# A transformer in one kernel: halves of a product placed by rule, rotary tables, a run of sums and the norms reordered

## The chip, the core and the metric

The kernel runs on one core of a Trainium2 chip. A core has TensorE (matmuls; PE in the rows, and PEld for its weight loads), VectorE (DVE), ScalarE (ACT), GpSimd (POOL) and SyncE (SP, which here only starts transfers); each works through its own queue of instructions in order and waits on semaphores. The metric is the device time of one execution in microseconds, the median of three runs.

## The reference

Two model blocks follow each other on 256 tokens of width 2048, all in fp32 from memory to memory; the output is the last layer norm's.

```python
def first_block(x, mem, ...):
    x = x + hybrid_mixer(x, ...)       # gated delta rule (8 heads) beside block attention (8 heads)
    x = x + cross_attention(x, mem, ...)
    x = x + conv_ffn(x, ...)           # (silu(conv(h @ w_gate) + b) * (h @ w_up)) @ w_down, d_ff 5632
    return rmsnorm(x, final_norm_g)

def second_block(x, positions, ...):
    cos, sin = _rope_tables(positions)
    for layer in range(2):
        if layer == 0:
            h = _mamba2_mixer(x, ...)  # in: 2048 -> 10304, 8 groups of a state-space model, out: 4096 -> 2048
        else:
            k_sh, v_sh = _shared_kv(x, kv_w, kv_b, cos, sin)
            h = _swa_mixer(x, k_sh, v_sh, cos, sin, ...)   # 32 heads of 64, window 128, rotary part of 16
        x = _layernorm(ALPHA * x + h, ln_g[layer], ln_b[layer])
    return x

def _rope_tables(positions):
    inv_freq = ROPE_THETA ** (-jnp.arange(0, ROT_DIM, 2, dtype=jnp.float32) / ROT_DIM)
    ang = positions.astype(jnp.float32)[..., None] * inv_freq
    return jnp.cos(ang), jnp.sin(ang)
```

## The kernel before

**Tiling.** Activations lie transposed in SBUF, as tiles of 128 features x 256 tokens (`XT[:, m, :]`). A weight matrix is read in chunks of 128 output features x 1024 rows, eight blocks k of 128 rows. SP loads a chunk into WR; ScalarE rounds it into WH (L1244); VectorE writes the rest, WR - WH, into WL (L1661). The moving operand is held the same way as XH and XL, or OH and OL. `half_of` then issues three matmuls for each block k, 128x128 weights against 128x256: L784 (XH, WH), L785 (XL, WH), L786 (XH, WL). There are 6144 such blocks, 18432 of the 20814 matmuls. The other matmuls are small steps between them: norms, transposes, attention, the state-space model's inner products.

**A split.** At the places in `OPENED`, 16 that are written out by hand, `in_two` issues the first matmul of a block as two with 128 columns (L760, L761). All 16 stand in some block of a stretch of products.

**The order.** `make_plan` writes one list of steps, and each engine issues its share of every step in that list's order. `product` appends the halves of a product, four blocks each, and after each calls `slot`, which takes a step from each small task that is due; `begin(task, names, gap, first)` enters such a task, with `gap` slots between its steps and `first` slots ahead. ScalarE's and VectorE's work on chunk i stands a fixed three chunks ahead of its use (AHEAD = 3).

**The program in order**, with the names of the products: gq, gk, gv, gz (delta rule), mq, mk, mv (attention), wo; xkv, xq, xo (cross attention); fg, fu, dn (feed-forward: 44 of fg and fu by turns, dn in four parts); a norm and dt; for each of eight groups g of the state-space layer sb, sc, x0 to x3, z0 to z3 and the steps "ssm" g (cb, x0, x1, ds, ..., y1, ns, nr); so, in four parts: 0 and 1 behind groups 2 and 4, 2 and 3 behind group 7; layer norm 0 with bkv (`three`); then 16 times wg and wq, one of each for a tile ti, beside the steps "swa" of tile ti - 1 (rope, lg, sm, sn, bk, pv); bo in two parts; layer norm 1 and the store.

**The steps that the change touches.** "rot" makes the rotary tables: seven steps on VectorE (L2238 to L2253 are five of their lines) and two Sin activations on ScalarE (L1562), begun ahead of so part 2; the tables lie in T2(0) and the scratch in T1(4) to T1(6) and T2(1). "mid" 1 sums the layer's input over its 16 tiles for the statistics: GpSimd copies (L2447) and adds (L2450), one in each slot from bkv 3 on, then "s". The rope of a product wq ti is four VectorE instructions (L2331) and two of GpSimd (L2637, L2640), and TensorE's attention of that tile (L1207, L1208) waits for them. "ln" is a layer norm: statistics ("stat"), TensorE's "sub", "rows" and "more", then "pair" 0 to 7, in which VectorE scales two tiles each (L2317). Some pairs get their mean subtracted ahead: in `centred` by VectorE (L2276, 128x512, for pairs 2, 8 and 14), by GpSimd for 10 and 12, and by TensorE for 4 and 6 (ln "sub"). In layer 0 ScalarE and GpSimd (L2630) also write XH and XL of the scaled tiles for the products bkv behind them.

## Time and profile before

| | |
|---|---|
| runs | 2455.44, 2456.77, 2457.15 us |
| median | 2456.77 us |
| the profiled execution | 2455.53 us, of which the span of the trace is 2453.5 us |
| busy | TensorE 98%, VectorE 72%, ScalarE 49%, GpSimd 21% |
| bytes moved | 418.29 MB, 170 GB/s |

Durations come from one profiled execution, which also marks when an instruction started and what the engine waited for. Matmuls are pipelined: the durations of TensorE's rows overlap, so what a matmul takes from the stream is the distance between two starts. The granted clock is the share of TensorE's full speed that the chip allowed.

### The profile page before, as it was taken

How to read it: one execution, taken by the hardware profiler on the slowest of the kernel's cores; microseconds unless marked ns; L12 is line 12 of the kernel's file. 1: busy time of each engine (PE TensorE's matmuls, PEld its weight loads, DVE VectorE, ACT ScalarE, POOL GpSimd, SP SyncE). 2: the span in 40 equal slices, each digit the busy share in tenths (PEclk: the TensorE clock that was granted, in tenths of full speed). 3: DMA queues.
4: the chain of work that ended last, by engine and by line, in shares of the span. 5: the costliest groups of instructions: out<-in, count | busy, mean ns of one | idle time of the engine just before them, and what ended most of it. 6: DMA issues, size and time to landing. Idle time of an engine off the chain costs nothing. (4 is left out here: it accounts for less than half of the span.)

```text
span 2453.5 us, 51551 instructions
## 1 busy us (share of the span) xinstructions
PE 2408.2 (98%) x20814; PEld 2367.7 (97%) x20814; DVE 1770.1 (72%) x2825; ACT 1211.1 (49%) x1918; POOL 505.7 (21%) x575
## 2 busy tenths in 40 slices
PE   7999999999999999999999999999999999999998
PEld 6999999999899999999999999999999999889998
DVE  6677646685666665655656888777887887888887
ACT  5433344554544444444444545544544554556554
POOL 1233310160200000000002312341221222521102
PEclk9999999999999999999999999999999999999999
DMA  6433335565555556556556645545554445444453
GB/s 216 157 126 123 123 125 178 186 205 168 163 189 192 197 177 209 195 179 211 191 179 190 195 161 170 172 165 171 171 178 158 163 151 183 151 154 157 157 166 117
DMA packets 124503, 418.29 MB, mean 170 GB/s; under 512 B 13796, under 2 KB 17644, under 8 KB 124012
## 3 DMA queue, kind: packets, MB, share of 16 engines
q1 hardware_dynamic: 124268, 415.00, 51.5%
q8 instruction: 167, 2.74, 0.5%
q14 instruction: 68, 0.56, 0.1%
HBM read 412.31 MB, written 3.68 MB: 170 GB/s over the span
## 5 line engine op out<-in xcount | busy, mean ns | idle before, releaser
L784 PE MATMUL b<-XH,WH 128*128 128x256 f32 x4213 | 1187.5, 282 | 21.9 <-DVE WL L1661 17.7
L785 PE MATMUL b<-XL,WH 128*128 128x256 f32 x4224 | 1173.9, 278 | 0.0
L786 PE MATMUL b<-XH,WL 128*128 128x256 f32 x4224 | 1173.3, 278 | 0.0
L1244 ACT ACTIVATE WH<-WR 128x1024 fp32r<-128x1024 f32 (+2 forms) x811 | 814.4, 1011 | 466.3 <-PE b L786 458.7
L1661 DVE TENSOR_TENSOR WL<-WR,WH 128x1024 fp32r<-128x1024 f32 (+2 forms) x811 | 993.3, 1235 | 14.5 <-ACT WH L1244 14.2
L784 PEld LDWEIGHTS b<-XH,WH 128*128 128x128 f32 x4213 | 793.4, 188 | 33.2 <-issue 17.0
L785 PEld LDWEIGHTS b<-XL,WH 128*128 128x128 f32 x4224 | 798.0, 189 | 0.6
L786 PEld LDWEIGHTS b<-XH,WL 128*128 128x128 f32 x4224 | 794.9, 188 | 0.0
L784 PE MATMUL b<-OH,WH 128*128 128x256 f32 x1675 | 468.4, 280 | 7.1 <-DVE WL L1661 5.7
L785 PE MATMUL b<-OL,WH 128*128 128x256 f32 x1680 | 466.5, 278 | 0.0
L786 PE MATMUL b<-OH,WL 128*128 128x256 f32 x1680 | 466.2, 278 | 0.0
L784 PEld LDWEIGHTS b<-OH,WH 128*128 128x128 f32 x1675 | 315.5, 188 | 10.6 <-issue 8.3
L785 PEld LDWEIGHTS b<-OL,WH 128*128 128x128 f32 x1680 | 316.0, 188 | 0.4
L786 PEld LDWEIGHTS b<-OH,WL 128*128 128x128 f32 x1680 | 315.8, 188 | 0.0
L1849 DVE TENSOR_TENSOR XT<-XT,b 128x256 f32<-128x256 f32 x192 | 80.5, 420 | 146.1 <-PE b L786 144.1
L1759 DVE SCALAR_TENSOR_TENSOR t1s<-cvs,par,t1s 128x256 f32<-128x256 f32 x304 | 153.0, 503 | 37.0 <-ACT t1s L1315 18.3
L1335 ACT ACTIVATE t1s<-t1s 128x256 f32<-128x256 f32 x156 | 64.8, 416 | 205.2 <-DVE t1s L1759 179.5
L2486 POOL TENSOR_TENSOR t2s<-t2s,RB 128x256 f32<-128x256 f32 x44 | 32.5, 739 | 559.9 <-DVE t2s L1787 559.9
L1807 DVE TENSOR_TENSOR cvs<-b,RB 128x256 f32<-128x256 f32 x116 | 48.7, 421 | 110.1 <-PE b L786 109.5
L2393 POOL TENSOR_TENSOR sms<-sms,con 128x2 f32<-128x2 f32 (+2 forms) x27 | 40.4, 1496 | 284.0 <-DVE sms L1980 98.0
L1787 DVE SCALAR_TENSOR_TENSOR t2s<-t1s 128x256 f32<-128x256 f32 x156 | 72.3, 464 | 8.3 <-ACT t1s L1335 8.3
L784 PE MATMUL b<-OX,WH 128*128 128x256 f32 x240 | 67.1, 279 | 0.0
(410 smaller groups left out, 2323.3 us busy)
## 6 DMA issues: line engine op xcount, KB each, us to landing
WR<-a_w_in SPq DMA_DIRECT2D x160, 512.0 KB, 3.7
WR<-w_in SPq DMA_DIRECT2D x112, 512.0 KB, 3.6
WR<-w_gate SPq DMA_DIRECT2D x88, 512.0 KB, 4.0
WR<-w_up SPq DMA_DIRECT2D x88, 512.0 KB, 4.1
WR<-a_w_out SPq DMA_DIRECT2D x64, 512.0 KB, 3.4
WR<-b_w_in SPq DMA_DIRECT2D x64, 512.0 KB, 3.7
WR<-w_down SPq DMA_DIRECT2D x64, 384.0 KB, 3.5
WR<-w_down SPq DMA_DIRECT2D x64, 320.0 KB, 2.9
```

What stands on the lines that cost most here:

```text
L784: mm(ps, WH[:, slot, at:at + P], xh, start=(k == 0), stop=False)
L785: mm(ps, WH[:, slot, at:at + P], xl, start=False, stop=False)
L786: m = mm(ps, WL[:, slot, at:at + P], xh, start=False, stop=(k == p["kt"] - 1))
L1244: act.activation(WH[:, s, 0:n], WR[:, r, 0:n], ACT.Copy).then_inc(*act_w.up(i))
L1335: act.activation(T1(2 + n % 2), T1(n % 2), ACT.Tanh, scale=0.5).then_inc(*act_cv.up("th", key))
L1661: dve.tensor_tensor(WL[:, s, 0:n], WR[:, r, 0:n], WH[:, s, 0:n].bitcast(F32), ALU.subtract).then_inc(*dve_w.up(i))
L1759: dve.scalar_tensor_tensor(y, b[:, j:j + S], pc(p["cw"], ci * K + j), y, ALU.mult, ALU.add).then_inc(*dve_cv.up("tap", key, j, also=("taps ...
L1787: dve.scalar_tensor_tensor(to, T1(2 + n % 2), 1.0, T1(n % 2), ALU.add, ALU.mult).then_inc(*dve_cv.up("end", key, also=("n", n)))
L1807: dve.tensor_tensor(cvs[:, p["c"] % 3, p["K"] - 1:p["K"] - 1 + S], ps, RB[:, :], ALU.mult).then_inc(*dve_ev.up(key))
L1849: dve.tensor_tensor(XT[:, m, :], XT[:, m, :], ps, ALU.add).then_inc(*dve_ev.up(key))
L2393: return pool.tensor_tensor(to[:, 0:n], columns[:, 0:n], cc("mhalf", 0, n), ALU.pow)
L2486: pool.tensor_tensor(gt[:, S:2 * S], gt[:, 0:S], RB[:, :], mult).then_inc(*pool_up.up(m))
```

## The change

**Splits.** `OPENED` goes. A new function `opened` reads the step list and puts one split into the second block of each stretch of product halves between small steps, if the stretch has at least 24 blocks, or at least 11 if the small step ahead of it is "ns", "sums" or a norm's. That gives 55 places, none of the old 16 among them.

**Rotary tables.** "rot" begins right behind norm 2, with a gap of 4, so its steps lie among the products fg and fu 0 to 3. The tables and the scratch move to parts of the constants that are no longer read (`turned`, "lev", "onehot"); so the waits at the first step are others.

**"mid" 1.** Gap 4 and first 24 in place of 1 and 1: a sum each product, from the loop of wg and wq on; "s" comes behind the last.

**Layer norms.** VectorE's `centred(8)` goes ahead, into "stat". GpSimd takes the root of the variance first and then its two sums, in layer 0 behind the XL parts of pairs 1 and 2. In layer 1 pair 14 gets its mean subtracted by TensorE, eight small matmuls (`ln`, "sub", 14), and `centred(14)` is gone there.

```diff
+        if layer:
+            self.step("ln", layer, "sub", 14)
...
-OPENED = {
-    (("gk", 0, 1), 4), (("gz", 1, 1), 12), (("gz", 2, 1), 12), (("gz", 3, 1), 12), (("xkv", 2), 8), (("fg", 0), 14),
-    (("fu", 0), 2), (("sc", 0), 8), (("x3", 0), 8), (("z1", 1), 4), (("z1", 4), 4), (("z1", 7), 4), (("so", 0, 14), 4),
-    (("so", 1, 14), 4), (("so", 2, 14), 4), (("bo", 0, 9), 4),
-}
...
+def opened(steps):
+
+    places, here, run, last = set(), None, 0, None
+    for step in [*steps, ("dt",)]:
+        if small(step):
+            sure = last is not None and (last[-1] in ("ns", "sums") or last[0] == "norm")
+            if here is not None and run >= (11 if sure else 24):
+                places.add(here)
+            here, run, last = None, 0, step
+        elif step[0] == "half":
+            key, k0, k1 = step[1], step[3], step[4]
+            if run == 0:
+                here = (key, k0 + 1)
+            run += k1 - k0
+    return places
...
     q.norm(2)
     q.late = False
+    q.begin(("rot",), ["a", "n0", "r0", "c0", "n1", "r1", "c1"], 4, 8)
...
-    q.begin(("rot",), ["a", "n0", "r0", "c0", "n1", "r1", "c1"])
...
-    q.begin(("mid", 1), [("x", m) for m in range(16)] + [None] * 12 + ["s"], 1, 1)
+    q.begin(("mid", 1), [("x", m) for m in range(16)] + [None] * 3 + ["s"], 4, 24)
...
-                if (key, k) in OPENED:
+                if (key, k) in plan.opened:
...
-            if m == 1:
-                w.wait_ge(*(pe_swa.of("lg", 15, 1) if layer else act_rot.of(1)))
+            if m == 1:
+                w.wait_ge(*(pe_swa.of("lg", 15, 1) if layer else pe_dt.of("t")))
...
                 centred(2)
+                centred(8)
...
-                    if 2 * j in (4, 6):
+                    if 2 * j in ((4, 6, 14) if layer else (4, 6)):
...
-                if j in (2, 5):
-                    centred(8 if j == 2 else 14)
+                if j == 5 and layer == 0:
+                    centred(14)
...
+                w.wait_ge(*dve_ln.of("ms", layer))
+                power(SM(21), SM(20)[:, 2:4], 2).then_inc(*pool_ln.up("r", layer))
                 w.wait_ge(*dve_ln.of("mu", layer))
-                for m in (10, 12):
...
+                if layer:
+                    centred(layer, 10)
+                    centred(layer, 12)
...
+                if j in (1, 2):
+                    centred(0, 8 + 2 * j)
```

In the order of the instructions, TensorE, behind the "nr" step of state-space group 4 (L747, in the changed kernel L778), where the stretch of 168 blocks begins; OH, OL are the moving operand's parts. Before:

```order
L786 MATMUL b<-OH,WL 128x256
L747 MATMUL b<-con,sms 128x128 x2
L784 MATMUL b<-OH,WH 128x256
L785 MATMUL b<-OL,WH 128x256
L786 MATMUL b<-OH,WL 128x256
L784 MATMUL b<-OH,WH 128x256
L785 MATMUL b<-OL,WH 128x256
L786 MATMUL b<-OH,WL 128x256
```

Now (L815 to L817 are L784 to L786, L791 and L792 are L760 and L761):

```order
L817 MATMUL b<-OH,WL 128x256
L778 MATMUL b<-con,sms 128x128 x2
L815 MATMUL b<-OH,WH 128x256
L816 MATMUL b<-OL,WH 128x256
L817 MATMUL b<-OH,WL 128x256
L791 MATMUL b<-OH,WH 128x128
L792 MATMUL b<-OH,WH 128x128
L816 MATMUL b<-OL,WH 128x256
L817 MATMUL b<-OH,WL 128x256
L815 MATMUL b<-OH,WH 128x256
```

The second block has its first matmul in two halves; the first block is as it was.

VectorE, in so part 2 behind the two t2s<-b,sms of group 7. Before:

```order
L2167 TENSOR_TENSOR t2s<-b,sms 128x512
L2238 SCALAR_TENSOR_TENSOR t1s<-t1s 128x256
L2240 SCALAR_TENSOR_TENSOR t1s<-t1s 128x256
L2242 SCALAR_TENSOR_TENSOR t1s<-t1s 128x256
L1849 TENSOR_TENSOR XT<-XT,b 128x256
L2249 TENSOR_SCALAR t1s<-t1s 128x256
L2251 TENSOR_TENSOR t1s<-t1s 128x256
L2249 TENSOR_SCALAR t1s<-t1s 128x256
L2251 TENSOR_TENSOR t1s<-t1s 128x256
L2253 TENSOR_SCALAR t1s<-t1s 128x256
L1661 TENSOR_TENSOR WL<-WR,WH 128x1024
```

Now the steps stand in the feed-forward stage, here between the low parts of the weights (WL, L1692) of fg and fu 1 to 3:

```order
L2269 SCALAR_TENSOR_TENSOR con<-con 128x256
L2271 SCALAR_TENSOR_TENSOR con<-con 128x256
L2273 SCALAR_TENSOR_TENSOR con<-con 128x256
L1692 TENSOR_TENSOR WL<-WR,WH 128x1024 x2
L1838 TENSOR_TENSOR cvs<-b,RB 128x256
L1707 TENSOR_TENSOR OL<-t2s,OH 128x256
L2280 TENSOR_SCALAR con<-con 128x256
L2282 TENSOR_TENSOR con<-con 128x256
L2280 TENSOR_SCALAR con<-con 128x256
L2282 TENSOR_TENSOR con<-con 128x256
L2284 TENSOR_SCALAR con<-con 128x256
L1692 TENSOR_TENSOR WL<-WR,WH 128x1024
```

Seven instructions of the same kinds, now with feed-forward steps in place of so's beside them, and on `con` in place of `t1s`.

GpSimd, between the ropes of the shared keys and those of wq (L2637, L2640; now L2674, L2677). Before:

```order
L2637 TENSOR_TENSOR t1s<-t1s,t2s 128x256
L2640 TENSOR_TENSOR t1s<-t1s 128x256
L2447 COPY ACC<-XT 128x256
L2450 TENSOR_TENSOR ACC<-ACC,XT 128x256 x14
L2637 TENSOR_TENSOR t1s<-t1s,t2s 128x256
L2640 TENSOR_TENSOR t1s<-t1s 128x256
```

Now:

```order
L2674 TENSOR_TENSOR t1s<-t1s,con 128x256
L2677 TENSOR_TENSOR t1s<-t1s 128x256
L2674 TENSOR_TENSOR t1s<-t1s,con 128x256
L2677 TENSOR_TENSOR t1s<-t1s 128x256
L2479 COPY ACC<-XT 128x256
L2482 TENSOR_TENSOR ACC<-ACC,XT 128x256
L2674 TENSOR_TENSOR t1s<-t1s,con 128x256
L2677 TENSOR_TENSOR t1s<-t1s 128x256
L2482 TENSOR_TENSOR ACC<-ACC,XT 128x256 x2
L2674 TENSOR_TENSOR t1s<-t1s,con 128x256
L2677 TENSOR_TENSOR t1s<-t1s 128x256
```

The 14 sums in a row are one or two between two ropes, and they begin two ropes later.

## Rows read from the trace of the kernel before

**Rows 1.** Page head, TensorE's waits over the span (us, times, longest)

```profile
span 2453.5 us, 51551 instructions
...
PE 2408.2 (98%) x20814; PEld 2367.7 (97%) x20814; DVE 1770.1 (72%) x2825; ACT 1211.1 (49%) x1918; POOL 505.7 (21%) x575
...
PE b L784 <- DVE WL L1661: 23.4, 10, 14.1
```

**Rows 2.** Windows of L785: stretch, us, busy (x count), clock, DMA share, GB/s

```profile
700.00:1300.00 600.00, 487.11 (x1765) 331.22 (x1766) 1.00 0.59 192
1802.50:1859.03 56.53, 44.96 (x160) 30.72 (x161) 1.00 0.55 185
2380.00:2432.99 52.99, 42.14 (x151) 28.16 (x150) 1.00 0.40 136
1498.00:1510.72 12.72, 10.12 (x36) 6.91 (x37) 1.00 0.54 184
```

**Rows 3.** TensorE's timeline at 663.4 (start, duration, group)

```profile
663.38 0.28 PE L784 MATMUL b<-XH,WH 128*128 128x256 f32 x1
...
663.72 0.22 PE L760 MATMUL b<-XH,WH 128*128 128x128 f32 x1
663.77 0.28 PE L761 MATMUL b<-XH,WH 128*128 128x128 f32 x1
663.89 0.33 PE L785 MATMUL b<-XL,WH 128*128 128x256 f32 x1
...
664.52 0.28 PE L784 MATMUL b<-XH,WH 128*128 128x256 f32 x1
```

**Rows 4.** The same timeline at 1416.3

```profile
1416.31 0.27 PE L761 MATMUL b<-XH,WH 128*128 128x128 f32 x1
1416.42 0.33 PE L785 MATMUL b<-XL,WH 128*128 128x256 f32 x1
```

**Rows 5.** TensorE's waits in 600:660

```profile
PE b L784 <- DVE WL L1661: 2.1, 2, 1.1
```

**Rows 6.** Windows of the so products' first and third part: each engine's busy time

```profile
1577.90:1621.40 43.50, 43.50 (x387) 42.06 (x386) 28.74 (x41) 19.87 (x26) 27.85 (x20) 1.00 0.47 156
1992.30:2040.00 47.70, 44.38 (x389) 42.63 (x387) 38.18 (x64) 25.16 (x32) 8.38 (x7) 1.00 0.44 144
```

**Rows 7.** TensorE's waits in 1992:2040; ScalarE's waits in 1990:2012

```profile
PE b L784 <- DVE WL L1661: 3.3, 2, 1.8
...
ACT t2s L1562 <- DVE t1s L2253: 8.4, 2, 4.3
```

**Rows 8.** Windows of the feed-forward stage and the sliding-window loop

```profile
662.00:1375.00 713.00, 713.00 (x6293) 713.00 (x6292) 454.51 (x644) 340.78 (x449) 66.06 (x117) 1.00 0.60 193
2180.00:2340.00 160.00, 160.00 (x1406) 150.86 (x1405) 143.66 (x311) 99.27 (x240) 28.66 (x24) 1.00 0.46 155
```

**Rows 9.** Timelines of GpSimd, VectorE, TensorE around 2140; last a window

```profile
2131.35 17.01 POOL L2450 TENSOR_TENSOR ACC<-ACC,XT 128x256 f32<-128x256 f32 x14
...
2140.90 3.50 DVE L2331 TENSOR_TENSOR t1s<-t1s,t2s 32x256 f32<-32x256 f32 x4
...
2149.89 0.50 PE L1207 MATMUL b<-KM,t1s 64*128 64x128 f32 x4 [3.05 <-POOL t1s L2640]
...
2151.00:2154.00 3.00, 3.00 (x16) 2.83 (x15) 1.02 (x2) 0.00 (x0) 0.00 (x0) 0.55 0.12 48
```

**Rows 10.** Timelines of VectorE, GpSimd at 2084; the page's group of L1661

```profile
2084.37 1.77 DVE L1661 TENSOR_TENSOR WL<-WR,WH 128x1024 fp32r<-128x1024 f32 x1
...
2084.19 0.86 POOL L2466 TENSOR_TENSOR ACC<-ACC,XT 128x256 f32<-128x256 f32 x1 [1.86 <-DVE XT L1849]
...
L1661 DVE TENSOR_TENSOR WL<-WR,WH 128x1024 fp32r<-128x1024 f32 (+2 forms) x811 | 993.3, 1235 | 14.5 <-ACT WH L1244 14.2
```

**Rows 11.** TensorE's waits in 2085:2130; VectorE's groups in 2444:2450

```profile
PE b L784 <- POOL XL L2630: 2.8, 4, 0.9
...
L2276 DVE TENSOR_TENSOR XT<-XT,t1s 128x512 f32<-128x512 f32 x2 | 1.4, 684 | 0.0
```

More of the change, by code:

```diff
@@ L369, with small @@
 MPLACE = list(range(16, 22)) + list(range(8)) + [8, 9]
+SMALL = {
+    "gdn": ("sums", "eg", "rows", "tv", "kk", "tt", "l0", "v0", "st", "xx", "v1", "o", "ns", "nr"), "att": ("lg", "v", "bk", "pv", "ns", "nr"),
+    "xat": ("lg", "tr", "o"), "ssm": ("cb", "x0", "x1", "ds", "st", "ec", "l0", "l1", "yo", "y0", "y1", "ns", "nr"),
+    "swa": ("lg", "bk", "pv"), "norm": ("sums", "rows"), "mem": ("tok", "rows"), "time": ("t",), "mid": ("s",), "toep": ("t",),
+    "ba": ("p", "b"), "kvt": ("t",), "vd": ("t",),
+}
+def small(step):
+    kind, name = step[0], step[-1]
+    if kind in ("dt", "ln"):
+        return True
+    return kind in SMALL and (name in SMALL[kind] or kind == "gdn" and name[0] in "ab")
+def opened(steps):
[12 more added lines that the diff above has]
+    return places
 def make_plan():
@@ L494, in make_plan @@
     q.steps = [s for s in q.steps if s[0] not in ("issue", "split") or s[1] < n + (s[0] == "split")]
+    q.opened = opened(q.steps)
     return q
@@ L604, in program @@
     ident, U, L, ones = cc("ident"), cc("U"), cc("L"), cc("ones")
+    turned = cc("lev", 0, 2 * S)
     spent = POFF["gdn_cw"][0]
@@ L1561, in rot @@
                 w.wait_ge(*dve_rot.of("c", which))
-                act.activation(T2(0)[:, half(which)], T1(6), ACT.Sin).then_inc(*act_rot.up(which))
+                act.activation(turned[:, half(which)], turned[:, half(which)], ACT.Sin).then_inc(*act_rot.up(which))
         def ln_square(layer, key):
@@ L2209, in rot @@
         def rot(name):
-            an, nn, rr = T1(4), T1(5), T1(6)
-            niv = T2(1)[:, 0:S].bitcast(I32)
+            an, nn = cc("lev", 2 * S, S), cc("onehot", 0, S)
+            niv = nn.bitcast(I32)
             two_pi = 2 * math.pi
@@ L2217, in rot @@
             which = int(name[1]) if len(name) > 1 else 0
+            rr = turned[:, half(which)]
             if name == "a":
-                w.wait_ge(*pe_ssm.of("nr", 6))
-                w.wait_ge(*act_os.of("ssm", 27))
-                w.wait_ge(*pe_dt.of("t"))
+                w.wait_ge(*pool_gdn.of("ao", 3, 6))
+                w.wait_ge(*pe_toep.of("t"))
                 w.wait_ge(*ld_pos.of("pos"))
@@ L2317, in ln @@
                     dve.scalar_tensor_tensor(XT[:, m, :], x, pc("ln_g", 16 * layer + m), rstd, ALU.mult, ALU.mult).then_inc(
-                        *dve_ln.up("b", layer, m, frees=frees if m in (3, 5, 7) else None))
-                if j in (2, 5):
-                    centred(8 if j == 2 else 14)
+                        *dve_ln.up("b", layer, m, frees=frees if m in ((3, 5, 7, 15) if layer else (3, 5, 7)) else None))
+                if j == 5 and layer == 0:
+                    centred(14)
                 if layer == 0:
@@ L2330, in rope @@
                 for i, o in ((a, a + 32), (a + 32, a)):
-                    last = dve.tensor_tensor(T1(9)[o:o + 32, :], source[i:i + 32, :], T2(0)[i:i + 32, 0:S], ALU.mult)
+                    last = dve.tensor_tensor(T1(9)[o:o + 32, :], source[i:i + 32, :], turned[i:i + 32, 0:S], ALU.mult)
                     last.then_inc(*dve_swa.up("u", o, *who))
@@ L2614, in ln, with centred @@
         def ln(layer, name, j=None):
+            def centred(layer, m):
+                pair = XT[:, m:m + 2, :]
+                pool.tensor_tensor(pair, pair, rep(T1(7), 2), add).then_inc(*pool_ln.up("sub", layer, m))
             if name == "stat":
@@ L2618, in ln @@
                     pool.tensor_scalar(SM(22)[:, 0:16], pc("ln_b", 0, 16), ALPHA, None, mult).then_inc(*pool_ln.up("b2"))
+                w.wait_ge(*dve_ln.of("ms", layer))
+                power(SM(21), SM(20)[:, 2:4], 2).then_inc(*pool_ln.up("r", layer))
                 w.wait_ge(*dve_ln.of("mu", layer))
-                for m in (10, 12):
-                    pair = XT[:, m:m + 2, :]
-                    w.wait_ge(*act_ln.of("sq", layer, 15))
-                    pool.tensor_tensor(pair, pair, rep(T1(7), 2), add).then_inc(*pool_ln.up("sub", layer, m))
-                    if m == 10:
-                        w.wait_ge(*dve_ln.of("ms", layer))
-                        power(SM(21), SM(20)[:, 2:4], 2).then_inc(*pool_ln.up("r", layer))
+                w.wait_ge(*act_ln.of("sq", layer, 15))
+                if layer:
+                    centred(layer, 10)
+                    centred(layer, 12)
             elif layer == 0 and name == "pair":
@@ L2636, in rope @@
                 w.wait_ge(*dve_swa.of("u", 64, *who))
-            pool.tensor_tensor(to, to if source is None else source, T2(0)[:, S:2 * S], mult).then_inc(*pool_swa.up("cos", *who))
+            pool.tensor_tensor(to, to if source is None else source, turned[:, S:2 * S], mult).then_inc(*pool_swa.up("cos", *who))
             w.wait_ge(*pool_swa.of("cos", *who))
```

## The prediction, made before the changed kernel ran

> **What bounds the kernel now.** I read the page's busy shares first. TensorE is busy for 2408.2 of 2453.5 us, 98% [rows 1], and the waits list says what the rest is: 23.4 us in 10 waits for the low parts of the weights (DVE WL), most of it, 14.1 us, in one wait, at the start, which the change does not touch [rows 1]. So a gain has to come from how fast TensorE streams, or from a few single waits. For the streaming I counted the second matmul of each three-matmul block in windows. In 700:1300 there are 1765 in 600 us, 339.9 ns a block; in 1802.5:1859.03 there are 160, 353.3 ns, and in 1498:1510.72 36, again 353.3 ns; 2380:2432.99 has 151 in 52.99 us, 351 ns [rows 2]. 
>
> **Part 1, the splits.** A split block has two matmuls of 128 columns where the first of 256 was. In mid-stream, from 663.72 to 664.52, six intervals take 0.80 us; six at the fast pace would be 0.68, six at the slow one 0.707 [rows 3]. So a split costs 0.12 us in a fast stretch and 0.10 in a slow one. What may it give? The pace behind it is what it was ahead of it at 663.72: the block from 663.38 to 663.72 took 0.34 us [rows 3]. That stretch was fast already, so it doesn't show that a split turns a slow one. At 1416, where a wait stood ahead, the second half and the next matmul are 110 ns apart (1416.31, 1416.42), and what follows is slow; at 663.77 to 663.89 it is 112 to 120 [rows 4, 3]. Of the 16 splits of before ten are followed by the fast pace and six by the slow one; the six are the first work after a small step or a wait. The new ones come one whole block later, when the stream already runs, which is like the case in mid-stream. I therefore take it that a stretch is fast from its new split on.
> Adding up: 55 places. 23 lie in stretches that are slow now, the longest of 168 blocks at 1801 and 164 at 2379, then 148 at 1392 (89 of them slow), 72 at 628 (44 slow), seven of 40 or 44 (one of them the 1498 of [rows 2]), twelve of 12 to 32; behind the splits 903 slow blocks x 13.2 ns = 11.9 us, minus 23 x 0.10: 9.6. 32 lie in stretches that are fast now: 32 x 0.12 = -3.8. The 16 old splits go: +1.7. In the stretches at 628, 1392 and 2108 TensorE waits for WL anyway (2.1 us in 600:660 [rows 5]), which takes back 1.0. Seven stretches of 16 blocks without a split, ahead of the "ds" step, are fast where the stretch before them is; at most 112 x 13.2 ns = 1.5 us, at least nothing, and I take 1.2. **Sum of part 1: 9.6 - 3.8 + 1.7 - 1.0 + 1.2 = 7.7 us.** The 8.2 us that are lost in slow stretches too short for a split stay.
> [...]
>
> **Part 2, the rotary tables.** Seven vector steps and two Sin activations leave the third part of the "so" products (1992 to 2040) for the first products of the feed-forward stage. The same steps without them, in the first part, take 43.50 us with TensorE busy for all of it; that part of 1992.3 to 2040.0 takes 47.70 with 44.38 busy and 64 vector instructions instead of 41 [rows 6]. Two waits for WL, 3.3 us in all, stand in it, and ScalarE, which must write WH ahead of WL, idles 8.4 us in 2 waits for DVE t1s L2253 of this chain [rows 7]. Bounds: nothing, if "so" products of part 3 wait by themselves, and 4.2 us, all of 47.70 - 43.50. I take the two waits and a little of the pace, near the upper end since these steps are all that differs: **+3.6**. What covers the steps at their new place: in 662:1375 TensorE is busy for 713.00 of 713 us, VectorE for 454.51 and ScalarE for 340.78 [rows 8], 36% and 52% free; weights stand some three chunks (8.2 us) ahead. The work that moves, 38.18 - 28.74 = 9.4 us of VectorE at most [rows 6] and a few table loads, lies in that slack. If the slack is gone, the bill is the same 3.3 us of waits, moved. On ScalarE the next gating of the feed-forward product is queued behind the waits for c0 and c1, with WH for the chunks behind it; that queue is what would be late.
>
> **Part 3, the burst of sums (mid 1).** GpSimd works without a pause for 17.01 us from 2131.35 on 14 sums; the rope products of wq 0 are queued behind them, and TensorE waits 3.05 us for them (2149.89) [rows 9]. Then its clock is low: 0.55 in 2151:2154, with 16 matmuls where 26 fit at 114 ns, 1.1 us lost [rows 9], and the eight small ones ahead of it lose 0.4 by the same ratio. 3.05 + 1.1 + 0.4 = 4.6. Now no sum stands ahead of this rope. It can come right behind VectorE's part (L2331, four in 3.50 us from 2140.90 [rows 9], so 2144.4), and its two steps of 0.72 end by 2146, before TensorE gets there (2149.89 - 3.05 = 2146.8). Next late would be VectorE, with 0.8 us to spare. **+4.6**; bounds 2.5 (half of the wait is left) and 4.6. The sums are now one each product in the sliding-window loop. There TensorE is busy for 160.00 of 160 us and VectorE for 143.66, 90%; GpSimd for 28.66 [rows 8]. A sum and a WL at the same time cost VectorE: 1.77 us where a GpSimd add of 0.86 ran beside it, against a mean of 1.235 [rows 10]. 16 sums x 0.54 = 8.6 us, out of 16.3 that are idle: -0.3 (0 to -4).
>
> **Part 4, the norms.** In layer 0 GpSimd's root comes before its sums, so the scaling starts earlier. GpSimd's sums now lie between the XL parts, on which four waits of 2.8 us in all ended [rows 11]. They may come half that earlier (+1.4) or a third later (-0.9): **+0.5**. In layer 1, at the end, two vector sums of 0.68 us stand between the last scalings (2 x 0.684 [rows 11]); one goes earlier, one goes to TensorE as eight small matmuls where it idles: 1.37 us at most. ScalarE's 16 closing steps run close behind VectorE's, so they are next: **+0.8** (0 to 1.4).
>
> **Sum**: 7.7 + 3.6 + 4.6 - 0.3 + 0.5 + 0.8 = 16.9 us. The profiled execution took 2455.53 us (2453.5 and 2 around it): 2438.6. The median of the runs, 2456.77, lies 1.2 above: 2439.9, I say **2440**. With the bounds of parts 2 to 4 its own range is 2434 to 2446.
>
> **The rivals.**
> A, a split only costs. Six splits of before are followed by slow stretches and no row shows one that turned. Then part 1 is -2.3 - 3.8 + 1.7 = -4.4, the sum 4.8, the time 2452. For: all that [rows 3] show is a price. Against: the splits in mid-stream are all followed by the fast pace. Chance 0.15. [...]
> B, VectorE becomes the bound in the sliding-window loop. 90% busy; the sums at 0.54 us each, half of them where TensorE is close behind: 4 us lost, 2444. Chance 0.08. The Trainium skill, "SBUF — State Buffer", section "Who interferes with whom", has a VectorE instruction with two SBUF operands and a GpSimd one block each other for the whole instruction; [rows 10] agree in sign, with 0.54 of 0.86 us.
> C, slower: the stretch of 2100 blocks of the feed-forward stage (661.6 to 1375.8), fast now with splits in its third block and at the start of fu 0, gets the slow pace. It has one split now, in its second block, and the moved rotary steps must not cause a wait in it: one would redraw the pace for all that is behind. Price 2098 x 13.2 ns = 27.7 us: 2440 + 27.7 = 2467. It outweighs the gain of 16.9 from 1280 slow blocks on, so a wait in its first 280 us decides ((2098 - 1280) x 0.34). Against: this stretch is fast before its split at 663.72 [rows 3], and the slack of [rows 8]. Chance 0.08.
> D, only some of the slow kinds turn (those after a wait don't): 5 us less, 2445. Chance 0.07.
>
> **How the numbers follow.** The forecast has 0.62. A measurement of this kernel can tell about 0.2%, 4.9 us, from no change. Faster by more: forecast, B, D and half of A (its 2452 lies on that line), 0.85; the other half of A is within: 0.07; C is slower: 0.08. The range: 2434 to 2452 holds the forecast, B, D and over half of A, and leaves out C and the tails.
>
> **What would show it.** In the trace of after, blocks behind a split at 1800 and 2370 are 340 ns apart (353: A). The third "so" part has no wait for WL and takes 43.5 us. GpSimd has no run of sums at 2130, the clock stays 1.00 there, and wq 1 takes 6.2 us. The feed-forward stage still takes 713 to 714 us; 741 is C. VectorE in the sliding-window loop is at 93 to 96% with no TensorE wait. What would make the forecast wrong is a pace that isn't set by what stands ahead of it, or one that the chip draws anew with each build.

## The result, and the profile after

The changed kernel takes 2472.04 us in the median of 21 runs (2445.33 to 2475.32) against 2455.44 us of the kernel before (21 runs, 2452.92 to 2457.75): a ratio of 1.0062, 95% interval 1.0053 to 1.0071. It is slower by 0.5 to 0.7%; the forecast was 2440 us. Twenty of the runs lie between 2469.5 and 2475.3, and one lies alone at 2445.33. That gap of 26 us is the heart of the case.

The head of the page of after, and the blocks of the feed-forward stage (L816 is L785 of before), the long stretch behind state-space group 4 and the last one, as windows of the second matmul of each block (columns as in [rows 2]):

```profile
span 2469.0 us, 51643 instructions
...
PE 2433.7 (99%) x20861; PEld 2394.5 (97%) x20861; DVE 1767.8 (72%) x2824; ACT 1212.5 (49%) x1918; POOL 505.5 (20%) x575
...
700.00:1300.00 600.00, 477.24 (x1700) 318.88 (x1700) 1.00 0.57 186
1831.00:1887.00 56.00, 45.50 (x165) 30.87 (x165) 1.00 0.58 189
2397.00:2450.00 53.00, 42.15 (x151) 28.15 (x150) 1.00 0.41 137
```

TensorE is busy for 2433.7 us, 25.5 more than in [rows 1], though it has only 47 matmuls more. In 700:1300 there are 1700 blocks where [rows 2] have 1765: 353 ns a block instead of 340, at a granted clock of 1.00 in both. The 168 blocks at 1831 do what was forecast: 165 in 56 us, 339 ns, where 1802.5:1859.03 of [rows 2] had 353. The 164 blocks at 2397 don't: 351, as before.

Laying the start of each stretch beside its start in the trace of before gives where the time went:

| part of the program | starts in before | in after | change of this part |
|---|---|---|---|
| delta rule to cross attention | 14.4 to 661.6 | 14.5 to 666.5 | +4.8 |
| feed-forward stage | to 1383.3 | to 1414.5 | +26.4 |
| state-space groups, so 0 and 1 | to 1992.6 | to 2018.9 | -4.9 |
| so part 2 | to 2044.3 | to 2066.6 | -4.0 |
| so part 3, layer norm 0, bkv | to 2131.2 | to 2152.9 | -0.6 |
| wq 0 to wq 2 (mid 1's old place) | to 2164.5 | to 2181.7 | -4.5 |
| sliding-window loop | to 2378.8 | to 2396.1 | +0.1 |
| last products and layer norm 1 | to 2453.5 | to 2469.0 | -1.8 |

Without the 26.4 of the feed-forward stage the sum is -10.9, and 2455.5 - 10.9 is 2444.6, close to the one run that lies alone, 2445.33.

**Where the stage turns.** Its 2100 blocks run at 340 ns up to fu 4, and from there, to the end of the stage, at 353.3. At the turn TensorE's timeline has one matmul late; the timeline of VectorE (DVE) beside it says why. After:

```profile
711.15 0.28 PE L816 MATMUL b<-XL,WH 128*128 128x256 f32 x1
711.26 0.28 PE L817 MATMUL b<-XH,WL 128*128 128x256 f32 x1
711.45 0.35 PE L815 MATMUL b<-XH,WH 128*128 128x256 f32 x1
711.64 0.28 PE L816 MATMUL b<-XL,WH 128*128 128x256 f32 x1
...
707.63 0.42 DVE L1898 SCALAR_TENSOR_TENSOR t2s<-b,t2s 128x256 f32<-128x256 f32 x1 [0.93 <-POOL t2s L2518]
707.97 0.28 DVE L2277 TENSOR_SCALAR con<-con 128x256 f32<-128x256 f32 x1
...
709.87 0.29 DVE L2284 TENSOR_SCALAR con<-con 128x256 f32<-128x256 f32 x1
710.08 1.22 DVE L1692 TENSOR_TENSOR WL<-WR,WH 128x1024 fp32r<-128x1024 f32 x1
```

Before, VectorE at the same place of the program, for the first chunk of fu 4, whose first matmul started at 706.68:

```profile
701.78 1.22 DVE L1661 TENSOR_TENSOR WL<-WR,WH 128x1024 fp32r<-128x1024 f32 x1
```

The starts are 110 to 120 ns apart up to 711.26; the next comes at 711.45, some 75 ns late, and the one behind it is late by as much again (711.64). It is the first matmul of fu 4, and the WL that it needs (L1692) runs from 710.08 to 711.30. Before, the same WL was written from 701.78 to 703.00, 3.7 us ahead of its use. In front of it now stand the six instructions of the rotary step c1, 707.97 to 710.08, which themselves came late, since L1898 had waited for GpSimd. The profile puts down no idle time to that matmul, because the durations of TensorE's rows overlap; it is seen only in the starts. 1967 blocks follow that wait at 13.2 ns more each: 26.0 us, for a wait that cost 0.15 us.

**The rest, line by line.** Windows of so part 2, of the sliding-window loop and of the feed-forward stage (columns as in [rows 6]), and the waits of TensorE in 2100:2150:

```profile
2019.00:2062.50 43.50, 43.50 (x389) 42.06 (x387) 30.37 (x41) 19.77 (x26) 9.99 (x8) 1.00 0.48 157
2180.00:2340.00 160.00, 160.00 (x1403) 151.11 (x1402) 145.86 (x311) 103.18 (x254) 46.20 (x40) 1.00 0.48 159
662.00:1402.00 740.00, 739.23 (x6291) 738.95 (x6291) 462.53 (x669) 346.17 (x455) 65.75 (x117) 1.00 0.58 186
...
PE b L815 <- POOL XL L2665: 3.2, 5, 0.9
...
2159.35 0.74 POOL L2674 TENSOR_TENSOR t1s<-t1s,con 128x256 f32<-128x256 f32 x1 [7.50 <-DVE t1s L1917]
2164.27 0.73 POOL L2677 TENSOR_TENSOR t1s<-t1s 128x256 f32<-128x256 f32 x1 [4.19 <-DVE t1s L2363]
```

So part 2 holds 389 matmuls in 43.50 us without idle time, as its first part did in [rows 6]; 47.70 are gone. The sliding-window loop has VectorE at 145.86 of 160 us, where [rows 8] have 143.66, and TensorE at 160.00 as there: the sums fit. GpSimd has no run of sums ahead of the ropes; its two rows, 2159.35 and 2164.27, are the rope of wq 0, which waits for VectorE, and the profile lists no wait of TensorE from 2150 to 2400. Around layer norm 0 the waits for GpSimd's XL are 3.2 us, against 2.8 in [rows 11].

### The profile page after: what moved, and what is told of

It reads as the page before. It is cut to its first block, busy times and chain, and to the rows that moved or that the text cites. A ratio compares the mean times of both kernels' runs of the same rounds, so it can differ in the third digit from the quotient of the medians.

```text
span 2469.0 us, 51643 instructions
## 1 busy us (share of the span) xinstructions
PE 2433.7 (99%) x20861; PEld 2394.5 (97%) x20861; DVE 1767.8 (72%) x2824; ACT 1212.5 (49%) x1918; POOL 505.5 (20%) x575
## 4 chain that ended last, share of the span: by engine, by line
PE 92%; DVE 3%; POOL 1%; ACT 1%; issue 1%; DMA 0%; POOLq 0%; SPq 0%; ACTq 0%; DVEq 0%
PE b L815 27%; PE b L816 27%; PE b L817 27%; PE b L785 2%; DVE WL L1692 1%; PE b L936 1%; PE b L949 1%; PE b L1172 1%; DVE t1s L1790 1%; PE b L778 1%; POOL t1s L2602 0%; POOL ACC L2433 0%; PE b L1253 0%; DMA XT<-xT 0%; POOL t1s L2458 0%
## 5 line engine op out<-in xcount | busy, mean ns | idle before, releaser
L815 PE MATMUL b<-XH,WH 128*128 128x256 f32 x4187 | 1185.9, 283 | 21.2 <-DVE WL L1692 16.7
L816 PE MATMUL b<-XL,WH 128*128 128x256 f32 x4224 | 1180.3, 279 | 0.0
L817 PE MATMUL b<-XH,WL 128*128 128x256 f32 x4224 | 1178.3, 279 | 0.0
L1692 DVE TENSOR_TENSOR WL<-WR,WH 128x1024 fp32r<-128x1024 f32 (+2 forms) x811 | 997.0, 1240 | 14.1 <-ACT WH L1275 13.8
L815 PEld LDWEIGHTS b<-XH,WH 128*128 128x128 f32 x4187 | 793.6, 190 | 32.3 <-issue 15.5
L816 PEld LDWEIGHTS b<-XL,WH 128*128 128x128 f32 x4224 | 795.9, 188 | 0.6
L817 PEld LDWEIGHTS b<-XH,WL 128*128 128x128 f32 x4224 | 796.2, 188 | 0.0
L815 PE MATMUL b<-OH,WH 128*128 128x256 f32 x1663 | 468.0, 281 | 3.3 <-DVE WL L1692 2.1
L816 PE MATMUL b<-OL,WH 128*128 128x256 f32 x1680 | 470.0, 280 | 0.0
L817 PE MATMUL b<-OH,WL 128*128 128x256 f32 x1680 | 469.1, 279 | 0.0
L815 PEld LDWEIGHTS b<-OH,WH 128*128 128x128 f32 x1663 | 314.7, 189 | 6.4 <-issue 4.4
L817 PEld LDWEIGHTS b<-OH,WL 128*128 128x128 f32 x1680 | 317.2, 189 | 0.0
L816 PEld LDWEIGHTS b<-OL,WH 128*128 128x128 f32 x1680 | 315.6, 188 | 0.4
L815 PE MATMUL b<-OX,WH 128*128 128x256 f32 x239 | 67.8, 284 | 0.0
```

Of the source, the lines that this page charges most:

```text
L815: mm(ps, WH[:, slot, at:at + P], xh, start=(k == 0), stop=False)
L816: mm(ps, WH[:, slot, at:at + P], xl, start=False, stop=False)
L817: m = mm(ps, WL[:, slot, at:at + P], xh, start=False, stop=(k == p["kt"] - 1))
L1692: dve.tensor_tensor(WL[:, s, 0:n], WR[:, r, 0:n], WH[:, s, 0:n].bitcast(F32), ALU.subtract).then_inc(*dve_w.up(i))
```

## The experiments

**The theory after the result** has two steps. W: the rotary steps at four slots make one WL late by a hair. R: any interruption of the stream draws TensorE's pace anew, a wait as well as a split or a small step, with odds that depend on the place; what is drawn then holds until the next draw. ("To draw" means here that the pace comes out as one of the two; whether chance has a part in it is not shown.) The rivals: the new split at fg 0, or the missing ones, made the stage slow (S); the table load or a rotary step does it, whatever the distance (T); or the pace is fixed by what the small step ahead left behind (K).

### The rotary steps farther apart (e1), back at their place (e2), and alone (e3)

```diff
-    q.begin(("rot",), ["a", "n0", "r0", "c0", "n1", "r1", "c1"], 4, 8)
+    q.begin(("rot",), ["a", "n0", "r0", "c0", "n1", "r1", "c1"], 12, 8)
```

> The changed kernel with the rotary steps 12 slots apart in the feed-forward stage instead of 4 (three products apart, not one). Theory W (at four slots they make VectorE's WL 75 ns late for fu 4, and that wait turns the remaining 1969 blocks of the stretch to the slow pace, 26 us): no wait, the stretch of 2100 blocks takes 714 us, and the time is 2445, as in the one run of 21 that took 2445.33. Rival S (the new split at fg 0, or the two old ones that are gone, set the slow pace): stays at 2472. Rival T (any ScalarE table load or rotary step beside the products does it): 2472 as well, with the turn at another block.

Measured: 2445.11 us in the median of 10 runs, ratio 0.9964 (0.9941 to 0.9986): the 26 us are gone. Nine runs lie from 2444.06 to 2446.86. The tenth, the profiled one, took 2472.88, and its trace has no late matmul in the stage; it is slow from the first blocks on:

```profile
700.00:1300.00 600.00, 477.14 (x1698) 318.79 (x1699) 1.00 0.56 185
```

1698 blocks in 600 us, 353 ns. There the draw at fg 0, behind norm 2 and its split, came out slow. So W holds for the usual run, and rival T is out, since the rotary steps still stand in the stage. R gets its first support: the pace is drawn at fg 0 too, slow in one run of ten here.

e2 is the changed kernel with `rot` begun ahead of so part 2, as it was before.

> The changed kernel with the rotary steps begun where they stood before, ahead of so part 2 (the tables still in the constants). Theory W: the feed-forward stretch is fast, the two waits for WL in so part 2 are back: 2445.3 + 3.8 = 2449. Rival S: 2472 + 3.8 = 2476.

Measured: 2449.79 us (6 runs, 2446.99 to 2452.09), 0.997 (0.9958 to 0.9981). The stage is fast, and in so part 2 the waits for WL are back, 3.6 us where [rows 7] have 3.3:

```profile
PE b L815 <- DVE WL L1692: 3.6, 2, 1.9
```

Rival S is out as the usual cause, since the splits at fg 0 are those of the changed kernel; in one run of e1 it is what happened. 2449.8 - 2445.1 = 4.7 us is what moving the steps is worth if nothing goes wrong; 3.6 were forecast. e3 is the kernel before with the rotary steps and tables moved and nothing else.

> The kernel before with the rotary steps and tables moved, all else as before. Here TensorE is one split (0.12 us) later at fu 4 than in the changed kernel, where VectorE was 0.075 us late. Theory W: it lies at the edge; either no wait and 2455.4 - 4.0 = 2451, or a wait and 2477, and whichever it is, the pace behind fu 4 goes with the wait. Rival S: 2451 and no slow pace even behind a wait.

Measured: median 2477.78 us of 10 runs, ratio 1.0057 (1.0024 to 1.009), and two groups: seven runs from 2476.85 to 2479.55, three from 2449.71 to 2454.32. The move alone makes the kernel slower by 21 us in the median, and its two outcomes lie 26 us apart. The profiled run is one of the three. Its timeline at fu 4 (L785 to L787 are here L784 to L786 of before), and the window of the stage:

```profile
706.21 0.28 PE L787 MATMUL b<-XH,WL 128*128 128x256 f32 x1
706.38 0.36 PE L785 MATMUL b<-XH,WH 128*128 128x256 f32 x1
706.57 0.28 PE L786 MATMUL b<-XL,WH 128*128 128x256 f32 x1
...
700.00:1300.00 600.00, 486.96 (x1765) 331.19 (x1765) 1.00 0.59 193
```

The late matmul is there (706.21 to 706.38, 170 ns, and 190 behind it), and yet the stage runs on fast, 1765 blocks in 600 us. "Whichever it is, the pace behind fu 4 goes with the wait" was wrong: the wait doesn't set the slow pace, it only lets the stream take a new one. Nor does the length of the wait put the outcomes in order: by the starts in the traces, the late matmul at fu 4 comes 166 ns behind the one before it in e7 (slow), 170 ns here (fast), 176 in e12 (slow) and 182 in after (slow). By their times seven of ten runs here and 20 of 21 of the changed kernel drew slow.

### The waits by themselves (e9)

```diff
             q.product(("fu", m), "w_up", m, 2, 16, "up", place=(part % 2) * 11 + i)
+            if m % 5 == 4:
+                q.step("pad", m, 8 + m % 4)
...
+        def pad(m, n):
+            lev = cc("lev", 0, 2 * S)
+            if m == 4:
+                w.wait_ge(*pool_gdn.of("ao", 3, 6))
+            for i in range(n):
+                dve.tensor_tensor(lev, lev, lev, ALU.max).then_inc(*dve_rot.up("pad", m, i))
+                w.wait_ge(*dve_rot.of("pad", m, i))
```

> The kernel before with extra VectorE work behind fu 4, 9, 14, 19, 24, 29, 34 and 39: 8 to 11 instructions on 128x512 that change nothing, so that WL comes late and TensorE waits eight times in the feed-forward stretch. Theory D (a wait draws the pace anew, mostly the slow one, each time): between the waits whole pieces of the stretch are at 340 or at 353 ns, slow in more than half, and at least one turns back to fast. Rival K (the first wait turns the stretch slow and it stays so): all pieces behind the first wait at 353. Rival U (waits of a microsecond or more don't slow it, only short ones): all at 340. The time is above 2456 by the waits, some 2 us each, and by 13.2 ns for each slow block.

Measured: 2501.26 us (2 runs), 1.0182 (1.0162 to 1.0203). TensorE waits eight times, 25.0 us in all. The added instructions (`pad`) stand on VectorE ahead of the next WL and change no value. TensorE's waits in the stage, the first of them in its timeline, a window behind it, and windows of the blocks (L787) behind the first, second, third, fourth and sixth wait:

```profile
PE b L786 <- DVE WL L1663: 25.0, 8, 4.1
...
719.73 0.36 PE L786 MATMUL b<-XH,WH 128*128 128x256 f32 x1 [2.11 <-DVE WL L1663]
...
720.60:723.60 3.00, 3.00 (x16) 3.00 (x16) 2.96 (x7) 0.73 (x2) 0.00 (x0) 0.50 0.84 228
...
724.00:774.00 50.00, 40.59 (x148) 27.60 (x148) 1.00 0.58 194
782.00:834.00 52.00, 41.36 (x148) 27.59 (x147) 1.00 0.58 190
844.00:896.00 52.00, 41.33 (x148) 28.28 (x148) 1.00 0.57 189
907.50:945.00 37.50, 30.36 (x110) 20.63 (x110) 0.99 0.54 166
1082.00:1134.00 52.00, 42.04 (x154) 28.81 (x153) 1.00 0.56 178
```

148 blocks in 50 us are 338 ns, 148 in 52 are 351. From the starts, the eight pieces behind the waits at fu 5, 10, 15, ..., 40 are at 340, 353.3, 353.3, 340, 340, 340, 353.3 and 340 ns a block. Three of eight are slow, which is less than half, but fast and slow follow each other freely: K and U fall, and so does the "mostly slow". Theory D holds in its core: each wait is a new draw. These waits are of 2.1 us and more, and behind seven of the eight TensorE's clock falls (0.50 in 720.6:723.6, with 16 matmuls in 3 us, which is the level of 1.2 GHz) for four to eight blocks before the pace is taken. The waits of 75 ns in the other kernels have no such fall. What the odds depend on isn't settled by this.

### A split in a running slow stream (e7, e12)

```diff
-    q.opened = opened(q.steps)
+    q.opened = opened(q.steps) | {(("fg", m), 1) for m in (6, 12, 18, 24, 30, 36, 42)}
```

> The changed kernel with seven more splits, in the second block of fg 6, 12, 18, 24, 30, 36 and 42, inside the feed-forward stretch that runs slow behind fu 4. Theory R (a split draws the pace anew wherever it stands): the stretch turns at some of the seven, and what is left of it is fast: with the first one turning, 2472 - 25 + 0.8 = 2448; with half of them, near 2460. Theory N (a split in a settled slow stream changes nothing, since only what stands ahead of a stretch or a wait sets the pace): 2472 + 7 x 0.10 = 2472.7, 353 ns a block on both sides of all seven.

Measured: 2445.71 us (4 runs, 2444.71 to 2447.47), 0.9957 (0.9942 to 0.9972), with the rotary steps at four slots and the late matmul at fu 4 as in the changed kernel. Windows of the blocks behind fg 6 and behind fg 12, and the timeline at fg 6 (L791 and L792 are the halves):

```profile
729.30:792.80 63.50, 51.54 (x187) 35.01 (x187) 1.00 0.58 193
794.70:858.20 63.50, 51.55 (x187) 35.01 (x188) 1.00 0.58 192
...
728.29 0.28 PE L815 MATMUL b<-XH,WH 128*128 128x256 f32 x1
728.41 0.28 PE L816 MATMUL b<-XL,WH 128*128 128x256 f32 x1
728.53 0.28 PE L817 MATMUL b<-XH,WL 128*128 128x256 f32 x1
728.64 0.22 PE L791 MATMUL b<-XH,WH 128*128 128x128 f32 x1
728.71 0.27 PE L792 MATMUL b<-XH,WH 128*128 128x128 f32 x1
728.82 0.34 PE L816 MATMUL b<-XL,WH 128*128 128x256 f32 x1
```

Ahead of the split the 49 blocks from fu 4 on are 353.3 ns apart by their starts (120, 120 and 110 ns in the rows); behind it 187 take 63.5 us, 340 each. The split turned the slow stream at once, and the six splits behind it left it fast. e12 has the first of the seven alone.

> The changed kernel with one more split, in the second block of fg 6, 49 blocks behind the short wait at fu 4, and nothing else changed. Theory R (a split in a running slow stream turns it): the wait stays, the stretch is slow for some 50 blocks and then fast, 2472.0 - 25.6 + 0.1 = 2446.5 in nearly every run. Rival (the seven splits of the earlier run were needed, or that was luck of four runs): runs at 2472 among them.

Measured: 2447.91 us (6 runs, 2444.41 to 2448.91), 0.9968 (0.9956 to 0.998). No run near 2472.

```profile
729.30:1300.00 570.70, 463.30 (x1679) 315.00 (x1679) 1.00 0.59 192
```

1679 blocks in 570.7 us, 339.9 ns. Ten runs of ten in e7 and e12 escape what 20 of 21 fell into. In the trace of e6 the split in the third block of the old list (fg 14) did the same behind six matmuls 117 to 119 ns apart; with fg 6 in e7, e12 and e11 (below) that makes four of four. (In before and e3 the starts were back at 113 or 114 ns ahead of fg 14, so these two show no turn.) Of 14 fast streams that met a split in full run in e7, e8 and e10, none turned slow. The one place of another kind is x3 0 of the old list, where a wait and a split come together: slow in four of five traces.

### The splits alone (e4), and where in the stretch (e8, e10, e11)

e4 is the kernel before with `opened` in place of the list.

> The kernel before with the splits placed by the rule, all else as before. As forecast (a stretch is fast behind its split): 2455.4 - 7.7 = 2447.7. Theory P (the pace behind a split is set by what stands ahead of the stretch, and the rule turns seven fast stretches of the first block slow, as the trace of the changed kernel shows: +4.8 there, -4.9 in the state-space stage, about -0.3 elsewhere): 2455. Rival S (the splits slow the feed-forward stretch): 2480.

Measured: 2455.74 us (10 runs), 0.9996 (0.9986 to 1.0005): 0.9 us less than before, which isn't told from nothing, where 7.7 us of gain were forecast. Theory P had 2455. Windows of wo 0,8 (164 blocks), the stage, sb 5 (168) and bo 0,11 (164) in e4; wo 0,8 in the kernel before (L785):

```profile
487.00:540.50 53.50, 42.58 (x152) 28.37 (x152) 1.00 0.61 200
700.00:1300.00 600.00, 487.07 (x1765) 331.22 (x1766) 1.00 0.58 192
1804.00:1860.00 56.00, 45.50 (x165) 30.87 (x166) 1.00 0.56 189
2380.00:2433.00 53.00, 42.15 (x151) 28.15 (x150) 1.00 0.40 135
...
484.50:538.00 53.50, 42.92 (x156) 29.15 (x156) 1.00 0.66 204
```

wo 0,8 was fast, 156 blocks in 53.5 us, and with a split in its second block it is slow, 152. The outcomes in the six traces of after, e1, e2, e4, e7 and e12, which have the rule's places:

| stretch, and the small step ahead of it | before | behind the split in the second block |
|---|---|---|
| z2 1, 2, 4, 6, 7 and sb 5 (nr) | slow | fast, 36 of 36 |
| z1 and so 14 (ns), eight stretches | 7 slow, 1 fast | fast, 48 of 48 |
| x3 and so 10 (y1), eight stretches | 7 fast, 1 slow | fast, 42 of 48 |
| mq, wo 0,1 (att v) | fast | fast, 18 of 18 |
| mv 1, 2, 3 and wo 0,8 (att nr) | fast | slow, 24 of 24 |
| xkv 2 (norm 1 rows) | fast, split in its first block | slow, 6 of 6 |
| bo 0,11 (swa 15 pv) | slow | slow, 6 of 6 |

The table has 31 of the 55 places. Of all 55, 42 have the same outcome in all six traces; the others, among them gz 0, wo 1,13, xkv 0, so 3,0 and wq 0, change from trace to trace. So the place decides mostly, not always.

The starts of the single matmuls say what the second block is. Behind the small step ahead of wo 0,8 they are 201, 117, 117, 123, 118 and 114 ns apart in the trace of before, and then 113 or 114: a stream needs some six matmuls to settle. The split of the second block is the fourth matmul. In the trace of after the starts there are 201, 117, 117, 174 and 172 ns apart (the two halves taken as one), and then 117 to 119. So this split meets a stream that hasn't settled yet. The places where it turned a fast stretch slow are of this kind, while no fast stream that had settled was turned by a split (14 of 14, above). Why the same split ends fast behind "nr" of the state-space groups isn't shown.

In e8 six splits that always failed stand in the seventh block, with the rotary steps 12 slots apart and the split at fg 6 added:

```diff
+    later = {(("mv", 1, 0), 5): (("mv", 1, 0), 10), (("mv", 2, 0), 5): (("mv", 2, 0), 10), (("mv", 3, 0), 5): (("mv", 3, 0), 10),
+             (("wo", 0, 8), 5): (("wo", 0, 9), 2), (("xkv", 2), 9): (("xkv", 2), 14), (("bo", 0, 11), 5): (("bo", 0, 12), 2)}
-    q.opened = opened(q.steps)
+    q.opened = {later.get(p, p) for p in opened(q.steps)} | {(("fg", 6), 1)}
```

> The changed kernel with the rotary steps 12 slots apart, one more split at fg 6, and in six stretches that stayed slow behind their split in every trace (mv 1, 2, 3; wo 0,8; xkv 2; bo 0,11) the split in the seventh block instead of the second. Theory M (a split turns a slow stretch once the stream has run for some blocks, as at fg 6): these six are fast from the seventh block on, 2445.2 - 6.1 = 2439. Theory K (what the small step ahead left behind fixes the pace, wherever the split stands in those stretches): wo 0,8 and bo 0,11 stay at 353 ns a block: 2445.

In e10 ten splits are gone:

```diff
+    not_here = {(("mv", 1, 0), 5), (("mv", 2, 0), 5), (("mv", 3, 0), 5), (("wo", 0, 8), 5), (("xkv", 2), 9), (("mq", 2, 0), 13),
+                (("mq", 3, 0), 13), (("wo", 0, 1), 5), (("x0", 1), 13), (("bo", 0, 11), 5)}
-    q.opened = opened(q.steps)
+    q.opened = opened(q.steps) - not_here | {(("xkv", 2), 8), (("fg", 6), 1)}
```

> The changed kernel with the rotary steps 12 slots apart, one more split at fg 6, and no split in ten stretches (mv 1, 2, 3; mq 2, 3; wo 0,1 and 0,8; x0 1; bo 0,11; in xkv 2 the old one in the first block): eight of them were fast without it in the trace of before. Theory: 6 x 0.12 of splits and 373 blocks x 13.2 ns come back: 2445.2 - 5.5 = 2439.7. Rival (these stretches draw the slow pace anyway, as the one behind swa 15 does): 2444.5.

In e11 all splits of the rule are in the first block:

```diff
-                here = (key, k0 + 1)
+                here = (key, k0)
```

> The changed kernel with the rotary steps 12 slots apart, one more split at fg 6, and every split of the rule in the first block of its stretch instead of the second. If it matters that the stream already runs when the split comes (the step of my forecast), the stretches behind ns, nr and y1, all fast now, fall back to the slow pace, 168 and 5 x 40 blocks among them: 2445.2 + 5 to 7 = 2451. Rival (only that there is a split matters): 2445.

Measured: e8 2440.62 us (4 runs), 0.9936 (0.9921 to 0.995); e10 2437.73 (4 runs, 2437.52 to 2438.14), 0.9924 (0.9909 to 0.9939); e11 2443.14 (4 runs), 0.9941 (0.9924 to 0.9957). Windows of wo 0,8 and bo 0,11 in e8, e10, e11, and in e11 of the stage ahead of fg 6 and behind it:

```profile
486.00:539.50 53.50, 42.92 (x156) 29.24 (x156) 1.00 0.64 206
2369.00:2422.00 53.00, 43.06 (x157) 29.30 (x156) 1.00 0.41 130
...
486.00:539.50 53.50, 42.87 (x156) 29.09 (x156) 1.00 0.66 207
2367.00:2420.00 53.00, 43.07 (x157) 29.29 (x156) 1.00 0.41 131
...
486.00:539.50 53.50, 42.88 (x156) 29.20 (x156) 1.00 0.65 204
2373.00:2426.00 53.00, 43.02 (x157) 29.28 (x156) 1.00 0.39 130
664.00:726.00 62.00, 49.34 (x176) 33.61 (x176) 1.00 0.55 181
728.00:1300.00 572.00, 464.35 (x1683) 315.80 (x1683) 1.00 0.59 193
```

156 or 157 blocks in 53 or 53.5 us: both stretches are fast in all three kernels. But e8 doesn't show what it was made for. All six stretches are fast in it from their first block, so the later split turned nothing, it only did no harm; and e10, with no split there except the old one in the first block of xkv 2, has them fast too and saves the splits. bo 0,11 had been slow in the kernel before with a split at bo 0,9 just ahead; the rule puts none there, the 16 blocks of bo 0,9 run slow, and bo 0,11 behind them fast. So what a stretch draws goes with the pace of the stretch ahead as well; the 16-block stretches behind "ds" had shown the same. e11 goes against the forecast's step: the first block serves as well as the second behind nr (sb 5 and the five z2 are fast) and better behind att nr, norm rows and pv, and it fails behind ns (seven of eight slow) and at fg 0 (176 blocks in 62 us, 352 ns, until the split at fg 6). "Fall back to the slow pace, 168 and 5 x 40 blocks among them" was wrong; it matters where, not that the stream already runs.

### The sums (e5) and the norms (e6), each alone

> The kernel before with the sums of mid 1 spread (gap 4, begun 24 slots on), all else as before. As forecast: 2456.6 - 4.6 + 0.3 = 2452.3. Rival (VectorE gets the bound from the sums beside its WL): less, down to nothing gained, with TensorE waits for WL in the sliding-window loop.

> The kernel before with the two layer norms' order changed, all else as before. As forecast: 2456.6 - 0.5 - 0.8 = 2455.3. From the trace of the changed kernel, where the last stretch gave back 1.9 us and layer norm 0 about 0.3: 2454.4. Rival: nothing, 2456.6.

Measured: e5 2451.04 us (10 runs) against 2455.66, 0.9977 (0.9968 to 0.9987), 4.6 us faster; e6 2454.79 (10 runs), 0.9996 (0.9987 to 1.0005), which isn't told from nothing. In e5 the profile lists no wait of TensorE from 2130 to 2370. Its window of the sliding-window loop, and TensorE's waits around layer norm 0 in e6:

```profile
2176.00:2336.00 160.00, 160.00 (x1405) 151.14 (x1406) 146.38 (x311) 103.20 (x251) 42.18 (x36) 1.00 0.47 154
...
PE b L786 <- POOL XL L2636: 3.5, 5, 1.1
```

VectorE has 146.38 of 160 us and TensorE 160.00, so rival B's cost doesn't appear. In e6 the waits for GpSimd's XL grow from 2.8 us [rows 11] to 3.5.

The medians of the four parts alone differ by 0.9 (e4), 4.7 (e2 against e1), 4.6 and 0.9 us, 11 in all, and e1, which has them all without the late matmul, is 11.5 faster than before. Each of these differences holds draws at other places too: in e6's trace 150 blocks from so 3,0 to bkv are slow where before had 39, 1.5 us.

## Why the prediction was wrong, point by point

**The step that failed is in part 2: "The work that moves [...] lies in that slack", and behind it "If the slack is gone, the bill is the same 3.3 us of waits".** Both halves failed. The slack was taken from shares, 36% of VectorE free over 713 us, and from "weights stand some three chunks (8.2 us) ahead". Ahead by that much was ScalarE's WH at best; VectorE's WL stood 3.7 us ahead at fu 4. Seven steps of up to 2.1 us within 40 us, at one each 5.44 us, took what VectorE gains back in that time (36% of 5.44 is 2.0), and its wait for GpSimd came on top. So it was late, by 75 ns. Then the bill was not the wait but the pace behind it: 26.4 us. Spacing of 12 slots takes the wait away (e1).

**Rival C** had this mechanism, its place and its price (27.7 us, measured 26.4; 2467 us, measured 2472), with a chance of 0.08. Two readings should have raised that. In the trace of before 6 of 16 splits and a quarter of all blocks are slow, so a new draw is no small risk; and whether the moved steps cause a wait was never worked out from the distance of one WL to its use. "A wait in its first 280 us decides" was right: it came 45 us in.

**Part 1** was forecast at 7.7 us and is worth 0.9 (e4), which isn't told from nothing. The price of a split was right: in e7 396 + 407 + 343 - 3 x 340 is 0.13 us in a fast stretch. The step "I therefore take it that a stretch is fast from its new split on" holds in the state-space stage, where the six stretches of 40 and 168 blocks turned 36 times of 36 (-4.9 us in that part of the program). It fails in the first of the two model blocks, where in the trace of after the same split left six fast stretches slow (mv 1 to 3, wo 0,8, xkv 2 and, in this trace alone, gz 0), 354 blocks, most of the +4.8 us, and at bo 0,11, which stayed slow (2.1 us of the sum). The premise behind it, "when the stream already runs, which is like the case in mid-stream", is what failed: the second block begins three matmuls into the stretch, and the stream isn't settled there. I had only ever priced two outcomes of a split in a fast stretch, 0.12 us or nothing; that it can turn it slow wasn't among my cases, though z1 and so 14 in the trace of before were slow behind theirs.

**Rival A**, a split only costs, is refuted by sb 5, z2 and fg 6. The Trainium skill, "TensorE: Matmul & The Clock Gate", section "Back-to-back issue gap", gives a stream of matmuls with weight loads one figure for each width, 81 ns at 128 columns and 131 ns at 512. It has no two paces; here every long stretch of 256-column matmuls at full granted clock, in all fourteen kernels, is at 113.4 or 117.8 ns, and the difference between the two is what decided this case.

**Part 3** was right in mechanism and size: 4.6 - 0.3 forecast, 4.6 measured (e5). Rival B didn't come. **The place of the rotary steps** gives 4.0 in so part 2 of the trace of after, and 4.7 between the medians of e2 and e1, where 3.6 were forecast with an upper bound of 4.2. **Part 4** was forecast at 1.3 and is 0.9 (e6), which isn't told from nothing. Two of its terms were off: layer norm 0 got worse (3.2 to 3.5 us of waits for XL against 2.8), and the end, from bo 0,11 on, takes 72.8 us in e6's trace against 74.7, 1.9 us of gain where the bound was 1.4. **Rival D** is nearest to what the splits do, with the wrong sign for part of them. **The range** is also wrong as a sum: the bounds of parts 2 to 4 as they stand give 2437.5 to 2451.5, not 2434 to 2446.

Added up: 11.5 us of gain where 16.9 were forecast (e1), and then 26.4 lost to one wait that the sum had at nothing.

## The version that beats both

e10 takes 2437.73 us, 0.9924 (0.9909 to 0.9939) of the kernel before and 34 us less than the changed kernel: the change with the rotary steps 12 slots apart, a split at fg 6 as insurance, some 180 blocks into the one long stretch, and without the splits at ten places, eight of which the trace of before shows fast without one. Its window of the stage:

```profile
700.00:1300.00 600.00, 487.53 (x1765) 331.35 (x1765) 1.00 0.59 193
```

Its four runs don't tell how often fg 0 draws slow, as in one run of e1; with the split at fg 6 that would cost 2.3 us instead of 28, as in the trace of e11.

## What to carry to other kernels

Where an engine runs a long stretch without a pause, ask of every edit near it whether it can cause a single wait there, and work that out from the distance between the last writer and its reader at that place, not from busy shares. If a short interruption can set the pace of all that follows, the price of a wait is the length of what follows, and a cheap second interruption some blocks on (here a product in two halves) bounds the loss. And try such a device class by class of places: the same split gained 2.1 us in one stretch (sb 5) and lost 1.6 in another (wo 0,8).

## What the runs showed of the hardware

- TensorE has two paces for 128x256 matmuls in a stream at full granted clock, 113.4 and 117.8 ns, and stays at the one it took: through 1967 blocks, some 5900 matmuls, in the trace of after. Behind a wait of 75 ns, a small step or a split of one matmul into halves it can be the other.
- At one place of a program the draw comes out mostly, but not always, the same way from run to run: 20 of 21 slow at fu 4 of the changed kernel, 7 of 10 in e3, one of 10 at fg 0 of e1. The median over few runs can hide 26 us of difference between executions of one program.
- Behind seven of eight waits of 2.1 us and more come four to eight blocks at 640 ns, at a granted clock of 0.50, the level of 1.2 GHz; then the clock is back and the pace is drawn (e9).
- Behind a small step the starts need some six matmuls to settle (201, 117, 117, 123, 118, 114, then 113 ns at wo 0,8). A split among these can leave the stream slow (24 of 24 behind "nr" of the attention); in a settled fast stream it never did (14 of 14), and it turned the slow stream of the feed-forward stage fast (four of four).
- What decides a draw is open. It goes with the kind of small step ahead, the pace of the stretch ahead and the block in which the split stands, and nothing in the profile shows the cause.
